# Token numbers of the expert slots from a DRAM table, tiles in pairs, an EPS column and moved work in a two-layer hybrid block

## The chip, the core and the metric

The kernel runs on one core of a Trainium2 chip. The metric is the device time of one execution in microseconds (us); less is better. Engines are named TensorE (PE in the rows; its weight loads are PEld), VectorE (DVE), ScalarE (ACT), GpSimd (POOL) and SyncE (SP). A "q" behind a name (ACTq) is the engine's own queue issuing something, such as a DMA.

## The reference

Input is a residual stream of 256 tokens of 1024 values, a conditioning vector, and the weights of two layers. All is float32. The layers have the same form, but the second one's channel part is a mixture of experts:

```python
def reference(x, c, ...):
    cond = silu(c)
    for l in range(2):
        sh_mix, sc_mix, gt_mix, sh_ffn, sc_ffn, gt_ffn = split(cond @ w_mod[l] + b_mod[l], 6)
        h = rms_norm(x, g_mix_pre[l]) * (1 + sc_mix) + sh_mix
        x = x + gt_mix * rms_norm(hybrid_mixer(h, ...), g_mix_post[l])   # two kinds of attention, 8 heads each
        h = rms_norm(x, g_ffn_pre[l]) * (1 + sc_ffn) + sh_ffn
        y = swiglu(h, w1, w3, w2) if l == 0 else moe_swiglu(h, w_router, w1, w3, w2)
        x = x + gt_ffn * rms_norm(y, g_ffn_post[l])

def moe_swiglu(h, w_router, w1, w3, w2):          # 8 experts, hidden width 3584
    top_v, top_i = top_k(h @ w_router, 2)
    combine = weights softmax(top_v) at top_i, else 0
    return sum(combine[:, e] * swiglu(h, w1[e], w3[e], w2[e]) for e in range(8))

def rms_norm(x, g):
    return x * rsqrt(mean(x * x) + EPS) * g
```

## The kernel before, in words

**Weights and products.** Weights come from DRAM in units of 1 MB into six `raw` buffers, issued by SyncE in a fixed order. Each unit is split into a high and a low part in float32r: ScalarE copies `raw` to `whi` (`split_hi`, L370), VectorE makes `wlo = raw - whi` (`split_lo`, L378), each in two halves of 128x1024. Three `whi`/`wlo` buffers turn round. TensorE forms every product from three (hi x hi, lo x hi, hi x lo: L1745, L1746, L1747 in `three`). Activations are split in the same way. SyncE may reload a `raw` buffer when VectorE has split what was in it.

**Order.** Each engine has its own program, written out by hand, and semaphores join them. An engine runs its program in order, so what stands behind a waiting instruction waits too. The stages are: first mixer, dense SwiGLU, second mixer, router, experts, final sum. Between stages, `transition` forms the RMS norms: ScalarE sums squares (`square_x`), GpSimd adds EPS (L1587) and raises to -1/2 (L1588, `rstd`), VectorE scales the rows (L935), TensorE transposes them (L1776).

**First stage.** For each of eight units, VectorE multiplies two halves of a modulation unit by the conditioning vector (`mod_columns`, L387), forms two coefficients (L952, L953), splits the unit's low part (L378 twice) and makes the low part of the hidden tile (`hlo`, L974) that TensorE's products with that unit need.

**Experts.** After the router, the work is cut into items: an item is one expert and up to 128 tokens. Eight items always run, and up to three more where an expert has over 128 tokens; in this run it is eight. Item 0 is written out, the others run in a loop whose count is read from memory. An item has seven blocks b of six units j: four for the two up products, two for the down product of the block before. In block b, ScalarE's `ffn_silu` (L777) and VectorE's `ffn_g` (L1260) make the hidden rows, TensorE transposes them (`hidden_T`, L2072) after unit 4.

**Tokens of an item.** `posI` holds, for each token and item, its slot. In block 2 of item n VectorE builds a 0/1 matrix of slots for item n+1 (`expert_slots`, L1377); in block 3 TensorE multiplies it with the token numbers (`slot_tokens`, L2252) and VectorE casts the result to `idx` (L1494). GpSimd then fetches the 128 rows of normed x from DRAM by `idx` (`fetch`, L1688). In blocks 4 and 5, TensorE transposes half of them each (`rows_T`, L2245), and ScalarE turns each half into four tiles of `h32e` (`tokens`, L854), between two unit splits.

**Sum.** An item's 128 output rows go to `y_rows` in DRAM (`store_rows`). In item 0 VectorE works out for each token the two rows of `y_rows` that are its own (`token_rows`, `ipair`, L1462); at the end GpSimd fetches them, and the last item is added from SBUF. Blocks of `y_rows` that no item may write are filled with zeros once, by a DMA that ScalarE issues (L868) after GpSimd has cleared its source (L1679).

## Time and profile before

| | |
|---|---|
| timed runs, median of 3 (lowest to highest) | 1620.96 us (1619.62 to 1623.14) |
| the profiled execution, its own time | 1618.41 us |
| its span, from first to last instruction | 1615.9 us |
| TensorE, VectorE, ScalarE, GpSimd busy | 1592.6, 1374.4, 1120.3, 142.8 us |
| expert items, 652 to 1560 us of the span | 908 us |

The profile is one execution of the program, so durations in it are compared with its own time, and only differences are carried over to the median. A busy share of TensorE says little by itself, since its products overlap; starts of instructions say more. "Idle before" names what ended the wait of an engine.

### The profile page before, as it was taken

Reading aid. Unit: us, or ns where it says so; the run is one execution under the profiler, and the core shown is the slowest. Engines: PE = TensorE matmul, PEld = TensorE weight load, DVE = VectorE, ACT = ScalarE, POOL = GpSimd, SP = SyncE. Lnnn points to the kernel's source line nnn. Section 1 sums busy time; section 2 is a strip of 40 time slices with the busy share of each in tenths; the row PEclk is TensorE's granted clock in tenths of the full one; section 3 lists DMA queues with packets and bytes.
Section 4 is the critical chain, followed back from the end, with each engine's and each line's share of the span. In section 5 each row is a group of like instructions: output and inputs, shape, how many; then the busy total and the mean of one; then the engine's idle time right before and its main releaser. Section 6 shows DMA issues by size and latency. Waiting matters only on the chain.

```text
span 1615.9 us, 23399 instructions
## 1 busy us (share of the span) xinstructions
PE 1592.6 (99%) x7726; PEld 1313.2 (81%) x7726; DVE 1374.4 (85%) x1661; ACT 1120.3 (69%) x1392; POOL 142.8 (9%) x214
## 2 busy tenths in 40 slices
PE   8999999999999999999999999999999999999997
PEld 7977878888789788788888888888888888888885
DVE  8888867787678767989988989989989989889898
ACT  5657544444456665778778778778878788788784
POOL 1030010000002100820000000000000000000071
PEclk9999999999999999999999999999999999999999
DMA  9966457777469453999999999999999999999993
GB/s 384 414 251 231 182 234 296 278 285 270 173 255 370 157 183 120 395 386 370 389 367 375 389 370 366 391 364 374 396 365 369 391 373 367 392 370 372 383 417 122
DMA packets 76409, 522.65 MB, mean 323 GB/s; under 512 B 9332, under 2 KB 10557, under 8 KB 14910
## 3 DMA queue, kind: packets, MB, share of 16 engines
q1 hardware_dynamic: 73522, 512.31, 81.7%
q0 software_dynamic: 1728, 6.29, 1.0%
q10 hardware_dynamic: 1100, 3.28, 0.5%
q8 instruction: 35, 0.57, 0.1%
q14 instruction: 24, 0.20, 0.0%
HBM read 513.97 MB, written 7.88 MB: 323 GB/s over the span
## 4 chain that ended last, share of the span: by engine, by line
PE 88%; DVE 4%; ACT 3%; issue 3%; POOL 0%; DMA 0%; DVEq 0%; ACTq 0%; POOLq 0%
PE ps L1745 27%; PE ps L1747 27%; PE ps L1746 27%; PE ps L2072 2%; DVE wlo L378 1%; ACT whi L370 1%; ACT vals L854 1%; DVE qk L1260 1%; PE ps L1800 1%; PE ps L1952 1%; PE ps L2245 0%; PE ps L1776 0%; PE ps L1931 0%; DVE raw L387 0%; DMA qk<-in_g_rows 0%
## 5 line engine op out<-in xcount | busy, mean ns | idle before, releaser
L378 DVE TENSOR_TENSOR wlo<-raw,whi 128x1024 fp32r<-128x1024 f32 x863 | 1014.5, 1227 | 141.5 <-ACT whi L370 141.0
L370 ACT ACTIVATE whi<-raw 128x1024 fp32r<-128x1024 f32 x863 | 862.8, 1053 | 202.3 <-PE ps L1747 178.8
L1745 PE MATMUL ps<-whi,hhi 128*128 128x512 f32 x1552 | 615.4, 397 | 2.3 <-DVE wlo L378 1.4
L1747 PE MATMUL ps<-wlo,hhi 128*128 128x512 f32 x1552 | 605.1, 390 | 0.0
L1746 PE MATMUL ps<-whi,hlo 128*128 128x512 f32 x1552 | 604.7, 390 | 0.0
L1745 PEld LDWEIGHTS ps<-whi,hhi 128*128 128x128 f32 x1552 | 291.4, 188 | 66.7 <-issue 4.4
L1747 PEld LDWEIGHTS ps<-wlo,hhi 128*128 128x128 f32 x1552 | 291.3, 188 | 62.2
L1746 PEld LDWEIGHTS ps<-whi,hlo 128*128 128x128 f32 x1552 | 291.7, 188 | 58.6 <-issue 1.0
L1745 PE MATMUL ps<-whi,ohi 128*128 128x512 f32 x432 | 173.2, 401 | 0.0
L1747 PE MATMUL ps<-wlo,ohi 128*128 128x512 f32 x432 | 168.9, 391 | 0.0
L1746 PE MATMUL ps<-whi,olo 128*128 128x512 f32 x432 | 168.4, 390 | 0.0
L387 DVE SCALAR_TENSOR_TENSOR raw<-raw,condb 128x1024 f32<-128x1024 f32 x94 | 111.5, 1223 | 0.0
L1747 PEld LDWEIGHTS ps<-wlo,ohi 128*128 128x128 f32 x432 | 81.1, 188 | 17.7
L1745 PEld LDWEIGHTS ps<-whi,ohi 128*128 128x128 f32 x432 | 81.2, 188 | 15.7 <-issue 0.3
L1746 PEld LDWEIGHTS ps<-whi,olo 128*128 128x128 f32 x432 | 81.3, 188 | 15.5
L777 ACT ACTIVATE qk<-ps 128x512 f32<-128x512 f32 x68 | 40.1, 598 | 61.5 <-PE ps L1747 61.5
L1745 PE MATMUL ps<-hhi,whi 128*128 128x256 f32 x256 | 73.8, 288 | 2.3 <-DVE hlo L974 2.3
L1687 POOL TENSOR_TENSOR spare<-tokid 128x1 f32<-128x1 f32 x8 | 2.0, 250 | 826.3 <-DVE idx L1494 826.3
L1746 PE MATMUL ps<-hhi,wlo 128*128 128x256 f32 x256 | 73.1, 285 | 0.0
L1747 PE MATMUL ps<-hlo,whi 128*128 128x256 f32 x256 | 73.0, 285 | 0.0
L782 ACT ACTIVATE ohi<-ps 128x512 fp32r<-128x512 f32 x46 | 27.5, 597 | 42.5 <-PE ps L2072 42.5
L1260 DVE TENSOR_TENSOR qk<-qk,ps 128x512 f32<-128x512 f32 x68 | 45.8, 681 | 10.8 <-PE ps L1747 10.8
(272 smaller groups left out, 1060.2 us busy)
## 6 DMA issues: line engine op xcount, KB each, us to landing
raw<-in_w_moe SPq DMA_DIRECT2D x336, 1024.0 KB, 7.1
raw<-in_w_pre_moe SPq DMA_DIRECT2D x97, 1024.0 KB, 5.0
raw<-in_w_mod_units SPq DMA_DIRECT2D x47, 1024.0 KB, 7.4
y_rows<-qk SPq DMA_DIRECT2D x7, 512.0 KB, 8.2
y_rows<-wide ACTq DMA_DIRECT2D x1, 2048.0 KB, 14.7
x<-in_x SPq DMA_DIRECT2D x2, 512.0 KB, 4.2
raw<-in_w_mod_units SPq DMA_DIRECT2D x2, 512.0 KB, 6.2
raw<-in_w_pre_moe SPq DMA_DIRECT2D x2, 512.0 KB, 7.7
```

The lines of the kernel that those rows point to most:

```text
L370: nc.scalar.activation(whi[:, home(s), part], raw[:, slot(s), part], ACT.Copy).then_inc(hi_done, 1)
L378: nc.vector.tensor_tensor(wlo[:, home(s), part], raw[:, slot(s), part], whi[:, home(s), part].bitcast(F32), ALU.subtract).then_inc(lo_done, 1)
L387: nc.vector.scalar_tensor_tensor(tile, tile, 1.0, condb[:], ALU.mult, ALU.mult, accum_out=modT[:, m:m + 1]).then_inc(mod_done, 1)
L777: nc.scalar.activation(silu[:, c, :], bank[c][:], ACT.Silu).then_inc(silu_done, 1)
L782: nc.scalar.activation(out, bank[6 + c][:].rearrange("p (k t) -> p k t", k=4), ACT.Copy).then_inc(gh_done, 1)
L854: nc.scalar.activation(h32e[:, k, :], src, ACT.Identity, scale=A[:, k:k + 1], bias=modT[:, SH[3] + k:SH[3] + k + 1]).then_inc(h32e_done, 1)
L1260: nc.vector.tensor_tensor(hid[:, c, :], silu[:, c, :], bank[(2 if n == 2 else 1) + c][:], ALU.mult)\
L1745: nc.tensor.matmul(out, a_hi, b_hi, start=first, stop=False, **kw)
L1746: nc.tensor.matmul(out, a_lo, b_hi, start=False, stop=False, **kw)
L1747: return nc.tensor.matmul(out, a_hi, b_lo, start=False, stop=last, **kw)
L1800: ins = nc.tensor.matmul(out, h32[:, k, c * P:(c + 1) * P], raw[:, slot(s0), k * NB:(k + 1) * NB], start=k == 0, stop=False)
L2072: ins = nc.tensor.transpose(bank[6 + c][:, k * P:(k + 1) * P], hid[:, c, k * P:(k + 1) * P], ident[:])
```

## The change

It has several parts, and what is computed stays the same.

1. **Slot numbers.** GpSimd scatters the token numbers 0 to 255 (`tokI`, four indirect DMAs of 128 words) to a DRAM table `tok_rows`, at the rows that `ipair` names, and reads it back as `idx_all`, one column for each item. ScalarE clears the table before by a DMA. In the looped items `idx` is a copy of a column; `expert_slots` and `slot_tokens` remain for item 0. So that a column is an item, `y_rows` and the table are laid out by slot and then item: a store's rows lie 12 rows apart. The zero fill covers five blocks of items, not four.
2. **Tiles in pairs.** ScalarE makes the four `h32e` tiles of a half in two pairs, one behind unit 2's split and one behind unit 3's.
3. **EPS column.** `x` gets a column 1025 that holds 32 times the root of EPS, so that the sum of squares holds EPS and GpSimd's add before `rstd` goes (not for the first norm, nor for the second half of the tokens before the router, nor for the last).
4. **Router.** The copies of `gate` from PSUM go from VectorE to ScalarE, behind the first item's splits; TensorE's gate transposes go behind the logits and filler takes their place. The logits product repeats the 8 columns 16 times.
5. **First stage.** `hlo` stands between the two low halves of a unit; unit 1's two modulation rows stand around unit 0's second low half; the copy of `distb` goes to ScalarE.

```diff
-        x = sb("x", [P, C, D])
+        x_eps = sb("x", [P, C, D + 1])
+        x = x_eps[:, :, 0:D]
...
+        tokI = sb("tokI", [P, C], mybir.dt.uint32)
+        idx_all = sb("idx_all", [P, ITEMS + 1], mybir.dt.uint32)
+        tok_table = tok_rows.rearrange("(p i) o -> p (i o)", p=P)
...
-                sp.dma_start(y_rows.rearrange("(i p) d -> i p d", p=P)[p], yrow).then_inc(yrow_free, 16)
+                sp.dma_start(y_rows.rearrange("(p i) d -> i p d", p=P)[p], yrow).then_inc(yrow_free, 16)
...
-                nc.scalar.activation(scr, x[:, c, :], ACT.Square, scale=1.0 / 32, accum_out=ss[:, 4 + c:5 + c])\
+                nc.scalar.activation(scr, x_eps[:, c, :], ACT.Square, scale=1.0 / 32, accum_out=ss[:, 4 + c:5 + c])\
...
-            def tokens(item, half):
+            def tokens(item, half, pair):
...
-                for k in range(4 * half, 4 * half + 4):
+                for k in range(4 * half + 2 * pair, 4 * half + 2 * pair + 2):
...
             split_hi(act, MOE0 + LEAD)
+            act.wait_ge(yg_done, 12)
+            for half in range(2):
+                act.wait_ge(gps_done, 2 * 3 + half + 1)
+                nc.scalar.activation(gate[:, half * NB:(half + 1) * NB], bank[GATE_BANK[3] + half], ACT.Copy).then_inc(gate_sb, 1)
             act.wait_ge(zero_set, 1)
-            act.dma_start(y_rows[(E - 1) * P:ITEMS * P, :].rearrange("(i p) d -> p i d", p=P),
-                          first_rows[:, 0:1, :].broadcast_to([P, EXTRA + 1, D])).then_inc(zero_out, 16)
+            act.dma_start(y_rows.rearrange("(p i) d -> p i d", p=P)[:, E - 1:ITEMS + 1, :],
+                          first_rows[:, 0:1, :].broadcast_to([P, EXTRA + 2, D])).then_inc(zero_out, 16)
+            act.wait_ge(tok_set, 2)
+            act.dma_start(tok_table, idx_all[:]).then_inc(table_zero, 16)
...
-                        if b in (4, 5) and j == 2:
+                        if b in (4, 5) and j in (2, 3):
                             act.wait_ge(elo_done, n * 2 + 2)
-                            tokens(n + 1, b - 4)
+                            tokens(n + 1, b - 4, j - 2)
...
                     if k:
-                        split_lo(dve, k)
+                        split_lo(dve, k, halves=(0,))
                         dve.wait_ge(eb_done, k)
...
                     if k == 0:
                         quarter(1, hi_done, lo_done)
+                        mod_columns(dve, 1, rows=(0,))
                         split_lo(dve, 0, halves=(1,))
-                        dve.wait_ge(dist_ps, 1)
-                        nc.vector.tensor_copy(distb[:, 0:DIST], bank[5][0:HEADS, 0:DIST]).then_inc(dist_sb, 1)
-                    if k + 1 < KC:
-                        mod_columns(dve, k + 1)
+                        mod_columns(dve, 1, rows=(1,))
+                    else:
+                        split_lo(dve, k, halves=(1,))
+                        if k + 1 < KC:
+                            mod_columns(dve, k + 1)
...
-                        if (b, j) == (2, 1):
-                            if p is None:
-                                dve.wait_ge(gath_done, 2)
-                            expert_slots(n + 1)
-                        if (b, j) == (3, 1):
-                            dve.wait_ge(idx_ps, n + 1)
-                            nc.vector.tensor_copy(idx[:], bank[7][:, S:S + 1]).then_inc(idx_sb, 1)
+                        if p is None and (b, j) == (2, 1):
+                            dve.wait_ge(gath_done, 2)
+                            expert_slots(1)
+                        if (b, j) == (3, 1):
+                            if p is None:
+                                dve.wait_ge(idx_ps, 1)
+                                nc.vector.tensor_copy(idx[:], bank[7][:, S:S + 1]).then_inc(idx_sb, 1)
+                            else:
+                                dve.wait_ge(table_in, 16)
+                                dve.wait_ge(gath_done, n * 2 + 2)
+                                nc.vector.tensor_copy(idx[:], idx_all[:, bass.ds(p + 2, 1)]).then_inc(idx_sb, 1)
...
             fetch(0)
+            pool.wait_ge(pair_done, 1)
+            pool.wait_ge(table_zero, 16)
+            pool.wait_ge(spare_set, 1)
+            nc.gpsimd.tensor_tensor(spare[:], tokid[:, 0:1], tokid[:, 1:2], ALU.add).then_inc(spare_set, 1)
+            for i in range(2):
+                for c in range(C):
+                    nc.gpsimd.indirect_dma_start(tok_rows, bass.IndirectOffsetOnAxis(ap=ipair[:, i * C + c:i * C + c + 1], axis=0),
+                                                 tokI[:, c:c + 1], None).then_inc(table_out, 16)
+            pool.wait_ge(table_out, 16 * 2 * C)
+            nc.gpsimd.dma_start(idx_all[:], tok_table).then_inc(table_in, 16)
...
                 if c:
-                    gate_rows(3)
+                    keep_busy(4)
                     transposes(3, c)
                 for k in range(KC):
                     pe.wait_ge(h32b if k >= 4 else h32a, KC * 2 + 4 * c + 4)
-                    ins = nc.tensor.matmul(bank[4][:, c * E:(c + 1) * E], h32[:, k, c * P:(c + 1) * P], wrA[:, k, :],
+                    ins = nc.tensor.matmul(bank[4][:, c * P:(c + 1) * P].rearrange("p (a e) -> p a e", e=E),
+                                           h32[:, k, c * P:(c + 1) * P],
+                                           wrA[:, k, :].rearrange("p (a e) -> p a e", a=1).broadcast_to([P, P // E, E]),
                                            start=k == 0, stop=k == KC - 1)
             ins.then_inc(lg_done, 1)
-            keep_busy(7)
+            gate_rows(3)
+            keep_busy(3)
...
-                        if (b, j) == (3, 0):
-                            slot_tokens(n)
+                        if p is None and (b, j) == (3, 0):
+                            slot_tokens()
```

The change moves line numbers; before and after are shown apart. ScalarE's program in a looped item, from block 4's `ffn_silu` on, where L370 (after: L379) is a split and L854 (after: L867) the tiles of `h32e`. Before:

```order
L777 ACTIVATE qk<-ps 128x512
L370 ACTIVATE whi<-raw 128x1024 x2
L905 ISA
L851 ISA
L854 ACTIVATE vals<-ps,modT,A 128x128 x4
L362 REGISTER_ALU
L370 ACTIVATE whi<-raw 128x1024 x2
```

After:

```order
L379 ACTIVATE whi<-raw 128x1024 x2
L924 ISA
L864 ISA
L867 ACTIVATE vals<-ps,modT,A 128x128 x2
L371 REGISTER_ALU
L379 ACTIVATE whi<-raw 128x1024 x2
L867 ACTIVATE vals<-ps,modT,A 128x128 x2
```

One unit split now stands between the two pairs of tiles. The second place is VectorE's program in the first stage, where L378 (after: L387) is a low half and L974 (after: L993) makes `hlo`. Before:

```order
L378 TENSOR_TENSOR wlo<-raw,whi 128x1024
L980 COPY qk<-ps 8x383
L387 SCALAR_TENSOR_TENSOR raw,modT<-raw,condb 128x1024 x2
L952 TENSOR_TENSOR modT<-modT,colsM 128x2
L953 SCALAR_TENSOR_TENSOR A<-modT,colsB 128x1
L378 TENSOR_TENSOR wlo<-raw,whi 128x1024 x2
L974 TENSOR_TENSOR hlo<-eb,hhi 128x256
```

After:

```order
L397 SCALAR_TENSOR_TENSOR raw,modT<-raw,condb 128x1024
L387 TENSOR_TENSOR wlo<-raw,whi 128x1024
L397 SCALAR_TENSOR_TENSOR raw,modT<-raw,condb 128x1024
L971 TENSOR_TENSOR modT<-modT,colsM 128x2
L972 SCALAR_TENSOR_TENSOR A<-modT,colsB 128x1
L387 TENSOR_TENSOR wlo<-raw,whi 128x1024
L993 TENSOR_TENSOR hlo<-eb,hhi 128x256
L387 TENSOR_TENSOR wlo<-raw,whi 128x1024
```

The copy has left, a modulation row stands ahead of the low half of unit 0, and `hlo` ahead of unit 1's second low half.

## Rows read from the trace of the kernel before

**Rows 1.** Page, part 1: busy us, share of the span, instructions.
```profile
PE 1592.6 (99%) x7726; PEld 1313.2 (81%) x7726; DVE 1374.4 (85%) x1661; ACT 1120.3 (69%) x1392; POOL 142.8 (9%) x214
```

**Rows 2.** Stretches: start:end, us, busy us of each engine, PEclk, DMA share, GB/s.
```profile
652.00:1560.00 908.00, 906.81 (x4130) 746.48 (x4129) 819.79 (x811) 733.46 (x841) 64.35 (x81) 1.00 0.98 380
```

**Rows 3.** ScalarE's waits, 652 to 1560 us: total, times, longest.
```profile
ACT whi L370 <- PE ps L1747: 68.6, 145, 0.7
```

**Rows 4.** DMA issues, 650 to 1590 us: count, KB each, median us to landing.
```profile
raw<-in_w_moe SPq DMA_DIRECT2D x327, 1024.0 KB, 7.1
y_rows<-qk SPq DMA_DIRECT2D x7, 512.0 KB, 8.2
```

**Rows 5.** Waits of TensorE's weight loads (PEld), 650 to 1590 us.
```profile
PEld ps L2072 <- DVE qk L1260: 8.9, 17, 1.0
```

**Rows 6.** Timeline, a token place: start us, us, instruction, idle before.
```profile
1312.82 1.50 ACT L854 ACTIVATE vals<-ps,modT,A 128x128 f32<-128x128 f32 x4 [0.67 <-PE ps L2245]
...
1315.31 2.36 DVE L378 TENSOR_TENSOR wlo<-raw,whi 128x1024 fp32r<-128x1024 f32 x2 [1.71 <-ACT whi L370]
...
1317.87 0.39 PE L1747 MATMUL ps<-wlo,ohi 128*128 128x512 f32 x1
...
1318.32 0.42 PEld L2072 LDWEIGHTS ps<-ident,qk 128*128 128x128 f32 x4 [0.48 <-DVE qk L1260]
...
1319.05 0.39 PE L1746 MATMUL ps<-whi,olo 128*128 128x512 f32 x1
```

**Rows 7.** Timeline, the same transposes where nothing is late.
```profile
1351.82 0.39 PE L1747 MATMUL ps<-wlo,ohi 128*128 128x512 f32 x1
...
1352.50 0.39 PE L1747 MATMUL ps<-wlo,ohi 128*128 128x512 f32 x1
...
1353.40 0.40 PE L1746 MATMUL ps<-whi,olo 128*128 128x512 f32 x1
```

**Rows 8.** Timeline, around the slot product L2252 (between the two).
```profile
810.65 0.39 PE L1747 MATMUL ps<-wlo,hhi 128*128 128x512 f32 x1
...
811.56 0.40 PE L1746 MATMUL ps<-whi,hlo 128*128 128x512 f32 x1
```

**Rows 9.** Tiles idx and ipair: ns min/median/max, first and last start us.
```profile
L1494 DVE CAST idx<-ps x8: 149/153/157, 696.7 to 1532.3; 128x1 uint32<-128x1 f32 x8
...
L1462 DVE CAST ipair<-rpair x1: 163/163/163, 747.6 to 747.6; 128x4 uint32<-128x4 f32 x1
```

**Rows 10.** Timeline, the zero fill's issue and what follows.
```profile
648.04 0.42 ACTq L868 DMA_DIRECT2D y_rows<-wide  x1
...
648.56 2.00 ACT L370 ACTIVATE whi<-raw 128x1024 fp32r<-128x1024 f32 x2 [3.27 <-POOL wide L1679]
...
651.00 0.50 PE L1745 MATMUL ps<-whi,hhi 128*128 128x512 f32 x1 [1.03 <-DVE wlo L378]
```

**Rows 11.** Timeline, weight loads of the logits and of the filler.
```profile
632.42 1.86 PEld L2214 LDWEIGHTS ps<-wrA,vals 128*128 128x128 f32 x16 [0.32 <-ACT vals L625]
...
634.20 1.64 PEld L2206 LDWEIGHTS ps<-nones,ones 128*128 128x128 f32 x14
```

**Rows 12.** Timeline, first stage, unit 1.
```profile
19.50 2.36 DVE L378 TENSOR_TENSOR wlo<-raw,whi 128x1024 fp32r<-128x1024 f32 x2
...
22.34 0.35 PE L1745 MATMUL ps<-hhi,whi 128*128 128x256 f32 x1 [0.90 <-DVE hlo L974]
```

**Rows 13.** Timeline, GpSimd's adds (L1587) and those who wait.
```profile
198.34 0.86 PEld L1776 LDWEIGHTS ps<-ident,wide 128*128 128x128 f32 x8 [0.38 <-DVE wide L935]
...
437.14 0.22 POOL L1587 TENSOR_SCALAR ss<-ss 128x1 f32<-128x1 f32 x1 [2.68 <-ACT at L586]
...
438.83 0.86 PEld L1776 LDWEIGHTS ps<-ident,wide 128*128 128x128 f32 x8 [0.74 <-DVE wide L935]
...
448.99 2.36 DVE L378 TENSOR_TENSOR wlo<-raw,whi 128x1024 fp32r<-128x1024 f32 x2
...
450.35 1.07 POOL L1587 TENSOR_SCALAR ss<-ss 128x1 f32<-128x1 f32 x1 [3.18 <-ACT at L586]
```

More of the change, by code:

```diff
@@ L1058, in router_transition @@
                                                accum_out=ss[:, 6:7]).then_inc(sqh_done, 1)
-                for half in range(2):
-                    gate_take(3, half)
             def last_add(i):
@@ L1441, in token_rows @@
                 if step == 2:
-                    link(nc.vector.tensor_tensor(row, place, jrow[:].rearrange("p (c i) -> p c i", c=1)
-                                                 .broadcast_to([P, C, ITEMS]), ALU.add))
+                    link(nc.vector.scalar_tensor_tensor(row, place, float(ITEMS + 1),
+                                                        jrow[:].rearrange("p (c i) -> p c i", c=1)
+                                                        .broadcast_to([P, C, ITEMS]), ALU.mult, ALU.add))
                 if step == 3:
@@ L1504, in _ @@
                 .then_inc(wcur_done, 1)
-            dve.wait_ge(cur_done, more + 3)
+            dve.wait_ge(cur_done, 3)
             slots_of(cur[:, 0, :])
@@ L1571, in _ @@
             links[0] += 1
+            nc.gpsimd.memset(x_eps[:, :, D:D + 1], 32 * EPS ** 0.5).then_inc(eps_set, 1)
             pool.wait_ge(pool_link, links[0])
@@ L1580, in _, with inv_rms @@
             select(lower, ALU.is_ge, -1, 1, 0, 0.0).then_inc(const, 1)
-            def inv_rms(done, src, at_col, *add):
+            def inv_rms(done, src, at_col, *add, with_eps=False):
                 if add:
                     link(nc.gpsimd.tensor_scalar(src, src, add[0], EPS, ALU.add, ALU.add))
-                else:
+                elif not with_eps:
                     link(nc.gpsimd.tensor_scalar(src, src, EPS, None, ALU.add))
```

43 lines of the change are left out of this document (27 added, 16 removed).

## The prediction, made before the run

> **What bounds the kernel now.** I read the page first: TensorE is busy for 99% of the span, VectorE for 85% [rows 1]. So what counts is TensorE's own work and the short gaps in it. The table of stretches puts 908 of the 1615.9 us into the expert items and shows TensorE full there, VectorE at 90%, ScalarE at 81%, and the DMA engines at 0.98 [rows 2]. The last figure asks whether the weight stream is the real bound. The list of waits answers no: ScalarE, which is the first to read each landed weight, waits in that stretch in six groups, all for TensorE, the largest being that for free whi buffers [rows 3]. No group names a DMA. A 1 MB load lands in 7.1 us [rows 4]; it is issued once unit s-6 has been split, about five unit periods of 2.8 us (1.05 MB at 380 GB/s [rows 2]) before ScalarE wants it. That leaves some 6 us.
>
> Then TensorE's gaps in the items: its weight loads wait for `ffn_g` (L1260) 17 times, 8.9 us in all, longest 1.0 [rows 5]. The timeline of one such place says why [rows 6]. ScalarE waits 0.67 us for the transposed rows, makes four h32e tiles in 1.50 us, and only then splits the next unit. VectorE's lo half of that unit starts after an idle of 1.71 us, `ffn_g` is queued behind it, and TensorE's hidden transposes load 0.48 us late.
>
> **The change part by part.** The sum is made against the profiled execution, 1618.41 us (span 1615.9), which lies 2.55 us under the median of the timed runs.
>
> *Token tiles in pairs.* What a gap costs is read from starts. From the last L1747 before the transposes to the L1746 behind them it is 1319.05-1317.87 = 1.18 us where `ffn_g` was late [rows 6], and 1353.40-1352.50 = 0.90 where it was not [rows 7]. So a listed idle of 0.48 costs 0.28; 0.20 of it is no loss. After the change two tiles stand ahead of the split, not four: half of 1.50, so the split, the lo half and `ffn_g` come 0.7 us earlier, 0.2 to 0.25 ahead of need. The other two tiles stand behind that split, so the split that follows them starts when it does now, and nothing is late next. Of the listed 8.9 us, 8.9-17x0.20 = 5.5 is real. One of the 17, in item 0, is at no token place and stays (0.3), and of the longest, 1.0, which the 0.7 doesn't cover, 0.1 stays: **-5.1 us**. Bounds: 0 (the lead is used up by something else) and 5.5.
>
> *Slot numbers from the table.* Item 0 keeps its product. In the seven looped items (y_rows is stored seven times [rows 4]) TensorE loses L2252. From L1747 to the L1746 behind it are 811.56-810.65 = 0.91 us [rows 8]; without it these are two steps of 0.227 us, a third of 1352.50-1351.82 [rows 7]. 7x(0.91-0.45) = **-3.2 us**; bounds 2.8 and 3.4. VectorE also loses a copy and two compares an item; it waits for ScalarE there, so I count nothing. What the table adds is on GpSimd's queue, behind the fetch for item 1: one small add, four scatters of 128 words, one read. GpSimd starts when `ipair` is ready, at 747.6; the first looped `idx` is wanted an item after the first, at 696.7+119.4 = 816 [rows 9]. No row shows a scatter of words. The 512 KB store lands in 8.2 us [rows 4]; four such in a row and a read are 41 us, which leaves 27. GpSimd's next fetch is queued behind them, and it too is wanted at 816 only. Cost 0, and to VectorE, which would wait, it costs only what goes beyond that.
>
> *A second DMA issue on ScalarE.* The zero fill of y_rows is issued at 648.04 in 0.42 us; before its next split ScalarE has been idle for 3.27 us, for GpSimd's memset, and TensorE then waits 1.03 us for the unit behind it [rows 10]. The table's clearing is issued in the same place: **+0.5 us** (0.42 and a gap). Bounds: 0, and 1.5 if five blocks take longer to issue than four. The two gate copies that move to ScalarE lie in the 3.27 us idle; without that cover they would cost their own length, which I put near the 1.50 us of the four tiles of [rows 6], the nearest row. Their reader on TensorE comes a block later.
>
> *Router.* The gate copies leave VectorE, but L1352, behind them, waits for the logits anyway. The logits product writes 128 columns for 8. The filler products of 128 columns took 1.64 us for 14 weight loads, the logits 1.86 for 16 [rows 11]: 0.117 each, so the loads pace both, and the width costs 0, at most 0.1. The gate transposes change places with filler: 0.
>
> *First stage.* TensorE waits 0.90 us for unit 1's `hlo`, which stands behind both lo halves, 2.36 together [rows 12]. Now it stands between them, 1.2 us earlier, so the gap goes. One mod row stands before unit 0's second lo half instead of behind it; that half is wanted only after two column blocks of products. The distb copy leaves VectorE. **-1.0 us**: the gap and a little fill. Bounds: 0 (that mod load lands late and holds VectorE, so that the unit after is late) and 1.1.
>
> *EPS column.* It removes one GpSimd add ahead of `rstd`. Where TensorE's loads wait 0.38 and 0.74 for the normed rows, less the 0.20 that is no loss, it gives 0.18 and, the add at 437.14 being 0.22 and its gap 0.08, 0.30 [rows 13]. The third add, at 450.35, took 1.07 us. But it ended just as VectorE's pair of L378 did, 448.99+2.36 = 451.35 [rows 13]: VectorE held it, and would hold the next GpSimd step in its place. So 0.2 there, not 1.1. **-0.7 us**, bounds 0 and 1.6.
> The Trainium skill says of this (page "SBUF — State Buffer", section "SBUF: two separate sides") that the two engines take a port pair as an exclusive lock for a whole instruction, and the loser blocks. By that rule the part is -0.7; by the add's length alone it would be -1.6.
>
> x[:, 1] now begins 4 bytes off. I count nothing for it; the last output transfer is the one place where it could show.
>
> Sum: -5.1-3.2+0.5-1.0-0.7 = -9.5 us. 1618.4-9.5 = 1608.9; against the timed median, 1620.96-9.5 = **1611.5 us**. Its own range goes from -11.6 (5.5, 3.4, 0, 1.1, 1.6) to -4.3 (half of the pairs, 2.8, 1.5 lost, half of the first stage): 1609.4 to 1616.7.
>
> **The rivals.**
> *The pairs don't free `ffn_g`.* The lead is 0.2 us, and the first pair still waits 0.67 us for the transposes. If VectorE has something else ahead of it, the waits stay: -9.5+5.1 = -4.4, 1616.6. For it: the small lead. Against: VectorE waited there for ScalarE, 1.71 us, and for nothing else.
> *The weight stream becomes the bound.* At 0.98 the DMA engines are nearly always busy [rows 2]. If they can't give more, an item stays as long as it is, and only the parts outside the items count: -1.0-0.7+0.5 = -1.2, 1619.8, no change. Against: no wait for a load in the stretch, 6 us in hand, and the demand rises by only 8.3/908 = 0.9%, from 380 to 384 GB/s.
> The Trainium skill's page "DMA: Bandwidth & Descriptors", section "Specifications", gives about 358 GB/s as one core's share of HBM. By that rule the stream would be over its limit already and this rival would hold, 1619.8; the trace disagrees, with 380 GB/s over 908 us.
> *Slower: the store with a stride.* y_rows is now slot-major, so a store writes rows of 4 KB that lie 48 KB apart. A store's share of the engines is 0.52 MB at 380 GB/s = 1.4 us. Free in an item are 2% of 119.4, 2.4 us, so it decides from 2.7 times the cost per row on. At four times it asks 4.2 more, 1.8 more than is free, in seven items: with the gain in the items gone too, 1620.96-1.2+12.6 = 1632. For it: the trace has no such store. Against: the packets stay 4 KB.
>
> **How the numbers follow.** Likeliest 0.68; pairs without effect 0.14; stream the bound 0.12; strided store 0.04; anything else 0.02. The predicted time is the first's, 1611.5. From 1607.5 (its low end and a run's spread, about 1.3 us under the median before) to 1617.5 (the first rival and the like) lie the first two cases, 0.82. A difference under 0.2% (3.2 us) can't be told from none: the first case and most of the second are faster, the third is the same. Faster 0.81, same 0.14, slower 0.05.
>
> **What would show each step.** Waits of TensorE's loads for `ffn_g` in the items: two or three for 17, under 2 us. No 128x1 product in looped items. An item of about 118.3 us for 119.4. TensorE starts unit 1 at about 21.3 us, not 22.34. The wait at 651 us is 1.5, not 1.03. At mixer 1's start `rstd` comes 0.2 to 0.3 earlier, its GpSimd row stretched by VectorE. I am wrong if ScalarE waits for raw in the items, if the waits for `ffn_g` stay, or if VectorE waits for the table.

## The result and the profile after

| | before | after |
|---|---|---|
| timed runs, median (lowest to highest) | 1620.3 us (1619.62 to 1623.14) | 1638.76 us (1638.3 to 1639.16) |
| span of the profiled execution | 1615.9 us | 1636.3 us |

The ratio is 1.0115, with a 95% interval from 1.0103 to 1.0127. The changed kernel is 18.5 us slower; the prediction was 1611.5 and faster, and the range ended at 1617.5.

First the page of the changed kernel, against [rows 1]: busy us, share of the span, instructions.

```profile
PE 1615.1 (99%) x7698; PEld 1310.0 (80%) x7698; DVE 1376.3 (84%) x1637; ACT 1121.6 (69%) x1395; POOL 152.0 (9%) x218
```

VectorE, ScalarE and the weight loads have the busy times of before to within 3.2 us. TensorE has 28 instructions fewer and 22.5 us more. The stretch of [rows 2] confirms it, now in the changed kernel:

```profile
652.00:1560.00 908.00, 906.57 (x4032) 732.78 (x4031) 808.71 (x782) 721.03 (x825) 65.40 (x91) 1.00 0.97 373
```

TensorE is as full as it was, at the same granted clock of 1.00, yet the stretch holds 4032 of its instructions where it held 4130. The DMA engines moved less, 373 GB/s for 380. So I looked for waits next. These are the ones of TensorE's weight loads in the changed kernel (the answer to [rows 5]; total, times, longest):

```profile
PEld ps L1781 <- DVE wlo L387: 1.9, 1, 1.9
PEld ps L2108 <- DVE qk L1279: 0.4, 1, 0.4
```

The 17 waits for `ffn_g` are one, where two or three were forecast. No wait has taken their place, and yet an item is longer: the tile `idx`, to be read beside [rows 9] (ns min/median/max, first and last start):

```profile
L1518 DVE COPY idx<-idx_all x7: 146/146/149, 823.6 to 1552.3; 128x1 uint32 x7
L1514 DVE CAST idx<-ps x1: 159/159/159, 703.3 to 703.3; 128x1 uint32<-128x1 f32 x1
```

(1552.3-823.6)/6 = 121.45 us an item for 119.4. What is left is the pace of the products themselves. The cleanest place is the dense SwiGLU, where the change moves nothing: 240 to 430 us, before,

```profile
240.00:430.00 190.00, 190.00 (x867) 157.23 (x866) 144.26 (x182) 77.99 (x89) 0.00 (x0) 1.00 0.74 279
```

and after:

```profile
240.00:430.00 190.00, 190.00 (x846) 153.63 (x845) 142.26 (x177) 77.77 (x89) 0.00 (x0) 1.00 0.73 276
```

TensorE never rests in either, and does 867 instructions in one and 846 in the other. The timeline of TensorE shows single products (start us, us; in `ps<-whi,hhi` the first name behind the arrow is the moving tile, the second the stationary one). Before:

```profile
901.67 0.39 PE L1745 MATMUL ps<-whi,hhi 128*128 128x512 f32 x1
...
903.48 0.39 PE L1747 MATMUL ps<-wlo,hhi 128*128 128x512 f32 x1
```

After:

```profile
901.67 0.39 PE L1782 MATMUL ps<-whi,hlo 128*128 128x512 f32 x1
...
903.53 0.40 PE L1781 MATMUL ps<-whi,hhi 128*128 128x512 f32 x1
```

Eight steps take 1.81 us before and 1.86 after. Over four windows of the trace (240 to 360, 700 to 760, 900 to 990, 1320 to 1410 us) I took the mean distance of the starts of consecutive 128x512 products, leaving out distances above 260 ns; this number is called **spacing** below. It is 227.3 to 227.7 ns before and 233.2 ns after, in every window. There are 3x1552 + 3x432 = 5952 such products, so 5.8 ns each are about 34.5 us, an estimate. The products with 256 columns did not slow down: behind the first 28 us of the trace they stand 119.9 ns apart before and 116.8 after, so a little closer. The weight loads take 188 ns both times.

The diff touches none of these products. What it does touch is where their operands lie in SBUF, the on-chip memory. `x` is allocated ahead of `hhi`, `hlo`, `ohi` and `olo`, and a row of it grew from 8192 to 8200 bytes, which the allocation rounds up to 8224. So all four stationary tiles (8192 bytes each) and all behind them lie 32 bytes further on, while `whi` and `wlo`, ahead of `x`, stay. Addresses in a partition, in bytes, as built:

| | whi | wlo | hhi | hlo |
|---|---|---|---|---|
| before | 65664 | 90240 | 127104 | 135296 |
| after | 65664 | 90240 | 127136 | 135328 |

### The profile page after: what moved, and what is told of

Its sections match the earlier page's. It is cut to its first block, busy times and chain, and to the rows that moved or that the text cites. A ratio compares the mean times of both kernels' runs of the same rounds, so it can differ in the third digit from the quotient of the medians.

```text
span 1636.3 us, 23335 instructions
## 1 busy us (share of the span) xinstructions
PE 1615.1 (99%) x7698; PEld 1310.0 (80%) x7698; DVE 1376.3 (84%) x1637; ACT 1121.6 (69%) x1395; POOL 152.0 (9%) x218
## 4 chain that ended last, share of the span: by engine, by line
PE 91%; DVE 3%; DMA 3%; ACT 1%; issue 1%; POOL 0%; ACTq 0%; DVEq 0%; POOLq 0%
PE ps L1781 29%; PE ps L1783 28%; PE ps L1782 28%; PE ps L2108 2%; DMA raw<-in_w_pre_moe 1%; DVE wlo L387 1%; DMA raw<-in_w_mod_units 1%; PE ps L1836 1%; ACT whi L379 1%; PE ps L1988 1%; DVE raw L397 0%; PE ps L2284 0%; PE ps L1812 0%; PE ps L1967 0%; DMA qk<-in_g_rows 0%
## 5 line engine op out<-in xcount | busy, mean ns | idle before, releaser
L387 DVE TENSOR_TENSOR wlo<-raw,whi 128x1024 fp32r<-128x1024 f32 x863 | 1020.2, 1229 | 150.3 <-ACT whi L379 149.3
L379 ACT ACTIVATE whi<-raw 128x1024 fp32r<-128x1024 f32 x863 | 864.4, 1052 | 219.5 <-PE ps L1783 194.0
L1781 PE MATMUL ps<-whi,hhi 128*128 128x512 f32 x1552 | 622.9, 401 | 2.3 <-DVE wlo L387 1.8
L1783 PE MATMUL ps<-wlo,hhi 128*128 128x512 f32 x1552 | 613.5, 395 | 0.0
L1782 PE MATMUL ps<-whi,hlo 128*128 128x512 f32 x1552 | 613.5, 395 | 0.0
```

The source lines that it names most:

```text
L379: nc.scalar.activation(whi[:, home(s), part], raw[:, slot(s), part], ACT.Copy).then_inc(hi_done, 1)
L387: nc.vector.tensor_tensor(wlo[:, home(s), part], raw[:, slot(s), part], whi[:, home(s), part].bitcast(F32), ALU.subtract).then_inc(lo_done, 1)
L1781: nc.tensor.matmul(out, a_hi, b_hi, start=first, stop=False, **kw)
L1782: nc.tensor.matmul(out, a_lo, b_hi, start=False, stop=False, **kw)
L1783: return nc.tensor.matmul(out, a_hi, b_lo, start=False, stop=last, **kw)
```

## The experiments

**Theory A**: the place of the stationary tiles against the moving ones sets the spacing; the parts of the change gave about what was forecast, and the 32 bytes took it and more. **Rival B**: the spacing follows from something that the change does (the second store layout, the table, x at odd places for its own readers), and the addresses are a coincidence. **Rival C**: the absolute alignment of a tile counts, not the distance between two.

### Where the tiles lie

The first four kernels share one edit, a tile `pad` that is never read, of 8 floats (32 bytes) unless said.

**e3_before_shift32** is the kernel before, with nothing else of the change:

```diff
+        pad = sb("pad", [P, 8])
         hhi = sb("hhi", [P, KC, S], F32R)
```

> The kernel before, with nothing but 32 unused bytes behind x. Theory A: 5952 x 5.4 ns = 32 us slower, about 1652 us, ratio 1.020, spacing 233 ns. Rivals B and C: no change, 1620.

Measured: 1645.33 us, ratio 1.0156 (1.0139 to 1.0173), spacing 233.2 ns. The same window as above, of this kernel:

```profile
240.00:430.00 190.00, 190.00 (x844) 153.56 (x843) 142.26 (x177) 78.18 (x89) 0.00 (x0) 1.00 0.73 277
```

32 unused bytes cost 24.6 us against the kernel before, and the window holds 844 instructions, 846 after the change. That ends rival B. The cost is under the estimate of 34.5 us. Set beside the trace of e6 below, which differs by the place of the pad alone, the distances between consecutive 128x512 products (5667 in e6, 5668 here) sum to 31.6 us more, the products with 256 columns give back 2.1, and the span is 25.8 longer. The rest, some 4 us, went into shorter waits and transposes. One such wait shows: the loads still wait for `ffn_g`, but 6.1 us in this kernel for the 8.9 of [rows 5]:

```profile
PEld ps L2073 <- DVE qk L1261: 6.1, 15, 0.5
```

**e4_before_shift32_behind** has the pad behind `olo`, so that only `wide`, `vals`, `qk` and the rest move.

```diff
+        pad = sb("pad", [P, 8])
         wide = sb("wide", [P, 2 * C * D])
```

> The kernel before, with the 32 unused bytes behind olo, so that hhi, hlo, ohi, olo (TensorE's stationary tiles) stay and wide, vals, qk and all later ones shift. If the stationary operand's address is the cause: no change, 1620. If it is traffic of the other engines on shifted tiles: about 1652.

Measured: 1619.94 us, ratio 0.9998 (0.9989 to 1.0008), spacing 227.3. So the move of `wide` and what follows costs nothing, and `hhi` to `olo` are left.

**e6_before_both32** has the pad ahead of `whi`: moving and stationary tiles shift together.

```diff
+        pad = sb("pad", [P, 8])
         whi = sb("whi", [P, SPLIT, UNIT], F32R)
```

> The kernel before with 32 unused bytes ahead of whi, so that moving and stationary tiles shift together by 32 bytes. If the distance between the two decides: no change, 1620, spacing 227.5. If the absolute address of the stationary tiles decides: 1645 as with the pad between them, spacing 233.

Measured: 1620.46 us, ratio 1.0 (0.999 to 1.0009), spacing 227.5. None of the six tiles lies where it did, and nothing is lost; `hhi` is at 127136, the very address that it has in e3. That ends rival C: the distance counts.

**e1_after_pad96** and **e2_after_pad32** ask the changed kernel how far is enough: pads of 96 and 32 bytes behind `x`, so that the tiles lie 128 and 64 bytes from their old place. e1 (e2 has 8 for 24):

```diff
+        pad = sb("pad", [P, 24])
         hhi = sb("hhi", [P, KC, S], F32R)
```

> The changed kernel with 96 unused bytes behind x, so that every tensor behind x starts again at a multiple of 128 bytes, as before the change. Theory A (the widened x moved all later tensors by 32 bytes, and TensorE's 128x512 products, whose stationary operand lies there, go from 227.5 to 233 ns apart): the spacing is 227.5 again, 5952 products give back 32 us, and the time is 1607 to 1610 us, ratio 0.992 to 0.994. Rival B (something the change computes or transfers slows TensorE): the time stays at 1638, spacing 233. Rival C (x[:, 1] off by 4 bytes slows its readers): stays at 1638 too.

> The changed kernel with 32 unused bytes behind x: later tensors start at odd multiples of 64 bytes. If theory A's grain is 64 bytes: 1607 to 1610 us like the 96-byte run. If it is 128 bytes: 1638, or between. Rivals B and C: 1638.

Measured: 1634.5 us (ratio 1.009, 1.0073 to 1.0106; spacing 232.4 to 232.8) with 128 bytes, and 1639.23 us (1.0119, 1.0102 to 1.0136; 233.3) with 64. My first idea, a line of 32, 64 or 128 bytes, was wrong.

**e13_before_shift256** is the kernel before with 256 bytes ahead of `hhi`.

```diff
+        pad = sb("pad", [P, 64])
         hhi = sb("hhi", [P, KC, S], F32R)
```

> The kernel before, with 256 bytes between x and hhi: all stationary tiles 256 bytes further from whi and wlo. Off by 32 and 64 bytes: 233.2 ns, by 128: 232.5 (in the changed kernel), by 512: 227.2. If the distance has to be a multiple of 256 bytes, 227.5 ns and 1620.4 us. If of 512 bytes: 232 ns and about 1640 us. If the effect fades with the distance: between, 229 to 231 ns, 1626 to 1635 us.

Measured: 1619.64 us, ratio 0.9999 (0.9989 to 1.0008), spacing 227.4. So the rule that fits all runs: a distance of a multiple of 256 bytes is good (256 more here, others in kernels below), and 32, 64 and 128 off are bad. Other remainders were not tried ahead of all four tiles. In the kernel before, whi to hhi is 61440 = 240x256.

### Which pair of tiles

**e14_shift_from_ohi** has the pad between `hlo` and `ohi`, **e11_shift_from_hlo** between `hhi` and `hlo`. **e15_only_hhi** puts `hhi` behind `olo`, with the pad ahead of it. **e16_only_wlo** puts the 32 bytes ahead of `wlo` and 224 behind it, so that `wlo` alone is off. The pads of e14, e11 and e16, and then the edit of e15:

```diff
+        pad = sb("pad", [P, 8])       # e14
         ohi = sb("ohi", [P, KC, S], F32R)
...
+        pad = sb("pad", [P, 8])       # e11
         hlo = sb("hlo", [P, KC, S], F32R)
...
+        pad = sb("pad", [P, 8])       # e16
         wlo = sb("wlo", [P, SPLIT, UNIT], F32R)
+        pad2 = sb("pad2", [P, 56])
         condb = sb("condb", [P, D])
```

```diff
-        hhi = sb("hhi", [P, KC, S], F32R)
         hlo = sb("hlo", [P, KC, S], F32R)
         ohi = sb("ohi", [P, KC, S], F32R)
         olo = sb("olo", [P, KC, S], F32R)
+        pad = sb("pad", [P, 8])
+        hhi = sb("hhi", [P, KC, S], F32R)
```

> The kernel before, with 32 bytes between hlo and ohi: only the stationary tiles of the down products, ohi and olo, are off (and wide and what follows, which e4_before_shift32_behind showed to be worth nothing). If a product is slow by the tiles that it and its neighbours use, the up products (hhi, hlo) stay at 227.5 ns and the down products (ohi, olo) go to 233: 1296 of 5952 products, 22% of the 24.5 us of e3_before_shift32, so 1620.4+5.3 = 1625.7 us (1624 to 1628). If any wrong tile slows all, 1645.

> The kernel before, with 32 bytes between hhi and hlo: hhi stays where it is, hlo, ohi, olo and what follows move by 32. If a product is slow when its own stationary tile lies wrong to its own moving tile, the products with hhi stay at 227.5 ns and those with hlo, ohi, olo have 233: the up products keep two thirds of their speed, the down products lose all, so two thirds of the 24.5 us of e3_before_shift32 or somewhat less: about 1633 us (1630 to 1637). If it is the load of the next stationary tile that collides with the stream that runs, the slow ones among the up products are those that precede a load from hlo, whatever their own tile. If only hhi's place matters, the time is that of the kernel before, 1620.5.

> The kernel before, with hhi moved behind olo and 32 bytes in front of it: hlo, ohi and olo lie at multiples of 4096 from whi, hhi does not; the mirror of e11_shift_from_hlo. If the load of a wrongly placed stationary tile disturbs the product that streams meanwhile, the intervals in which hhi is loaded (whi,hlo to wlo,hhi and wlo,hhi to whi,hhi) are slow and whi,hhi to whi,hlo stays fast, and the down products stay at 228 ns: spacing in the mean about 231 to 232, about 1636 us (1632 to 1642). If what counts is that the two stationary tiles in turn lie right to each other, the up products are slow by all three intervals, about 233 and 1640 us.

> The kernel before, with 32 bytes between whi and wlo and 224 bytes behind wlo: wlo is off by 32 to whi and by 224 to hhi, while whi to hhi is a multiple of 256. If 256 is a good distance (e13_before_shift256) and the stream of wlo is what a load then collides with, the products with wlo (a third) are slow and the others stay: about a third of 24.5 us, 1628 us (1626 to 1632). If only whi against the stationary tiles counts, 1620.4. If every wrong tile slows all, 1640 to 1645.

Measured: e14 1625.43 us (ratio 1.003, 1.0018 to 1.0041), e11 1647.45 (1.0163, 1.0147 to 1.0178), e15 1636.97 (1.0106, 1.0089 to 1.0122), e16 1638.09 (1.0112, 1.0095 to 1.0129). The timeline of the kernel before shows what goes on inside one interval, from one product's start to the next one's:

```profile
901.67 0.39 PE L1745 MATMUL ps<-whi,hhi 128*128 128x512 f32 x1
901.67 0.19 PEld L1746 LDWEIGHTS ps<-whi,hlo 128*128 128x128 f32 x1
901.90 0.39 PE L1746 MATMUL ps<-whi,hlo 128*128 128x512 f32 x1
```

The next product's stationary tile is loaded while the moving tile of the running one streams. The mean length of an interval by pair of products, over the whole trace, distances above 260 ns left out, in ns:

| interval | before | e3 | e11, hlo off | e15, hhi off | e16, wlo off | e14, ohi, olo off |
|---|---|---|---|---|---|---|
| whi streams, hlo loads | 227.6 | 233.3 | **238.3** | 230.6 | 229.6 | 227.4 |
| whi streams, hhi loads | 227.4 | 233.2 | 228.9 | **233.1** | 231.5 | 227.3 |
| wlo streams, hhi loads | 227.5 | 233.2 | 232.5 | **232.1** | **233.8** | 227.5 |
| whi streams, olo loads | 228.5 | 233.3 | **233.2** | 229.4 | 229.6 | **232.8** |

In bold stand the intervals in which the tile that streams and the tile that is loaded lie badly to each other (of e3 it is all four). Of the up products' three intervals, the one that rises most is a bold one in every kernel: by 10.7 in e11, 6.3 in e16, 5.7 in e15. A product's own stationary tile is not what counts, since in e11 the product with `hlo` has the fastest of the three (228.9). e14 is clean: up products keep their pace, down products lose 4.3 to 5.1 ns, and the time came within 0.3 us of what was expected. In the others the neighbours of a bad interval slow down too, by up to 5.0 ns in e11 (more than the 4.6 of a bad one in e15) and 4.1 in e16. So the mean rise over the three is 5.7 in e11, as in e3 where all lie badly, 4.4 in e15 and 4.1 in e16. The expectations for e11 (1633) and e16 (1628) counted bad pairs alone, and the times came out 14 and 10 us dearer. So the table points to TensorE's load of the next stationary tile meeting its own stream of the moving tile, and it doesn't show how a bad pair slows the interval behind it.

Do reads and writes of other engines take part? The traces at hand answer that. Take only the intervals in which ScalarE and VectorE are both idle throughout: 227.3 ns before (173 intervals), 233.1 after (183), and in e11 238.1, 228.6 and 232.5 in the order of the table's first three rows. That is the same as over all intervals. Nor is it the DMA engines. They stand still from 440 to 450 us, before and in e3:

```profile
440.00:450.00 10.00, 10.00 (x38) 6.77 (x36) 9.50 (x14) 7.36 (x13) 1.81 (x2) 1.00 0.00 0
440.00:450.00 10.00, 9.89 (x45) 7.37 (x44) 7.60 (x12) 7.49 (x13) 1.85 (x4) 1.00 0.00 0
```

and the consecutive 128x512 products there are 228.5 ns apart before (26 intervals) and 233.1 in e3 (30).

### The change with its tiles put right

**e5_x_behind** is the changed kernel with one allocation moved:

```diff
-        x_eps = sb("x", [P, C, D + 1])
-        x = x_eps[:, :, 0:D]
         hhi = sb("hhi", [P, KC, S], F32R)
...
         olo = sb("olo", [P, KC, S], F32R)
+        x_eps = sb("x", [P, C, D + 1])
+        x = x_eps[:, :, 0:D]
```

> The changed kernel with the wide x allocated behind olo. hhi, hlo, ohi, olo then lie 8192 bytes lower, so at the same place against whi and wlo modulo 8192 bytes, and only wide and all behind it stay shifted by 32. Theory A2 (what counts is where the stationary tiles lie against the moving whi and wlo, or against some large power of two, not their alignment to 32, 64 or 128 bytes; the 96-byte run left 232.4 ns): the spacing is 227.5 ns again and the time is what the prediction's sum gives, 1609 to 1612 us, ratio 0.993 to 0.995. Rival D (any move of the stationary tiles from where they were costs, by their absolute address): about 1635.

Measured: **1608.57 us**, ratio 0.9931 (0.9917 to 0.9944), spacing 227.2 to 227.5. The stretch of [rows 2] and the weight loads' waits:

```profile
652.00:1560.00 908.00, 908.00 (x4141) 751.59 (x4140) 826.49 (x796) 740.17 (x848) 83.34 (x86) 1.00 0.98 384
```

```profile
PEld ps L1781 <- DVE wlo L387: 3.9, 3, 2.1
PEld ps L2108 <- DVE qk L1279: 0.9, 1, 0.9
```

So the whole change is worth -11.8 us by the medians, and -9.7 by the two profiled executions (1618.41 and 1608.73). The kernel before scatters from 1618.3 to 1623.5 over all its timed runs, and its profiled execution lies at the low end; e12 below shows why.

**e9_condb_behind** also moves `condb` (4096 bytes) behind, which brings the tiles 4096 bytes nearer; **e10_ident_ahead** puts the 512 bytes of `ident` ahead of `hhi`. Both start from e5:

```diff
-        condb = sb("condb", [P, D])   # e9: from ahead of hhi to behind olo
         hhi = sb("hhi", [P, KC, S], F32R)
...
         olo = sb("olo", [P, KC, S], F32R)
+        condb = sb("condb", [P, D])
...
+        ident = sb("ident", [P, P])   # e10: from behind at2 to ahead of hhi
         hhi = sb("hhi", [P, KC, S], F32R)
```

> The kernel of e5_x_behind, but condb (4096 bytes, read only in the first stage and the modulation) is also taken out from between the weight tiles and the stationary tiles and stands behind olo: hhi to olo lie 4096 bytes nearer to whi and wlo, wide and what follows stay. If what counts is the distance modulo 4096 or less, the spacing of the 128x512 products stays 227.5 ns and the time is that of e5_x_behind, about 1608.6 us (1607.5 to 1610). If it counts modulo 8192, the spacing is 233 ns and the time about 1638. If a whole multiple of 8192 is better still than an odd multiple of 4096, the spacing falls under 227 ns, and each ns less is worth up to 6 us.

> The kernel of e5_x_behind, but the 512-byte tile ident stands ahead of hhi: hhi to olo and all up to ident's old place lie 512 bytes further from whi and wlo. Distances of 32 and 64 bytes off gave 233.2 ns, 128 off gave 232.5, both beside 227.5 for a multiple of 4096. If only the low bits up to 256 bytes count, this one is as fast as e5_x_behind, 1608.6 us (1607 to 1610.5). If the distance must be a multiple of 4096, it is slow: 232 to 233 ns, about 1634 to 1638 us. A value between, 229 to 231 ns and 1615 to 1628 us, would say that the effect fades with the distance.

Measured: 1608.6 us (ratio 0.9928, 0.9912 to 0.9943) and **1608.03 us** (0.9923, 0.9908 to 0.9938), spacing 227.3 and 227.2. Both are good distances; e10 is the fastest kernel of the study, by no more than can be told from e5.

### What each part is worth

Three kernels take one part out of e5. **e7_no_pairs** puts the four `h32e` tiles of a half back behind one split:

```diff
-                for k in range(4 * half + 2 * pair, 4 * half + 2 * pair + 2):
+                for k in range(4 * half, 4 * half + 4):
...
-                        if b in (4, 5) and j in (2, 3):
+                        if b in (4, 5) and j == 2:
```

> The x-behind kernel with all four h32e tiles ahead of the split again (part 2 of the change undone). By the prediction it is 5.1 us slower than the x-behind kernel and TensorE's loads wait some 15 times for ffn_g, 0.5 us each. If the pairs do nothing: the same as x-behind.

Measured: 1613.75 us, e5 plus 5.2 (ratio to before 0.9961, 0.9948 to 0.9974). The waits are back, as the wait row of this kernel shows:

```profile
PEld ps L2108 <- DVE qk L1279: 8.9, 16, 1.3
```

**e8_products_back** makes `idx` in every item by `expert_slots` and `slot_tokens` again; the table is still written and waited for.

```diff
-                        if p is None and (b, j) == (2, 1):
-                            dve.wait_ge(gath_done, 2)
-                            expert_slots(1)
+                        if (b, j) == (2, 1):
+                            if p is None:
+                                dve.wait_ge(gath_done, 2)
+                            expert_slots(n + 1)
...
-                                nc.vector.tensor_copy(idx[:], idx_all[:, bass.ds(p + 2, 1)]).then_inc(idx_sb, 1)
+                            nc.vector.tensor_copy(idx[:], bank[7][:, S:S + 1]).then_inc(idx_sb, 1)
...
-                        if p is None and (b, j) == (3, 0):
-                            slot_tokens()
+                        if (b, j) == (3, 0):
+                            slot_tokens(n)
```

> The x-behind kernel with the slot matrix and the product with the token numbers made in every item again and idx taken from them; the table is still written and waited for, but not read. By the prediction it is 3.2 us slower than the x-behind kernel (0.46 us in each of seven items). If the product was hidden: the same.

Measured: 1612.77 us, e5 plus 4.2 (ratio 0.9957, 0.9942 to 0.9973); by spans, 1609.9 and 1606.7, plus 3.2.

**e12_first_stage_back** undoes part 5 (ScalarE's copy of `distb` goes too):

```diff
-                        split_lo(dve, k, halves=(0,))
+                        split_lo(dve, k)
...
-                        mod_columns(dve, 1, rows=(0,))
                         split_lo(dve, 0, halves=(1,))
-                        mod_columns(dve, 1, rows=(1,))
-                    else:
-                        split_lo(dve, k, halves=(1,))
-                        if k + 1 < KC:
-                            mod_columns(dve, k + 1)
+                        dve.wait_ge(dist_ps, 1)
+                        nc.vector.tensor_copy(distb[:, 0:DIST], bank[5][0:HEADS, 0:DIST]).then_inc(dist_sb, 1)
+                    if k + 1 < KC:
+                        mod_columns(dve, k + 1)
```

> The kernel of e5_x_behind with part 5 of the change (first stage: hlo between the halves, modulation rows around, copy of distb on ScalarE) undone. The prediction's term for this part was -1.0 us. Then this kernel has 1609.6 us. If the part is what carried the 2.4 us that the other terms leave of the 11.8, it has 1610.5 to 1611. If the part is worth nothing, 1608.6.

Measured: 1610.94 us, e5 plus 2.4 (ratio 0.9937, 0.9924 to 0.9951). In the timelines of TensorE, unit 1 of the first stage starts in e12 at

```profile
22.59 0.55 PE L1777 MATMUL ps<-hhi,whi 128*128 128x256 f32 x1 [2.39 <-DVE hlo L991]
```

and in e5 at

```profile
21.18 0.36 PE L1781 MATMUL ps<-hhi,whi 128*128 128x256 f32 x1 [0.64 <-DVE hlo L993]
```

The stretch from 22.5 to 25.5 us, e12,

```profile
22.50:25.50 3.00, 2.91 (x14) 2.94 (x14) 2.90 (x7) 1.64 (x3) 0.00 (x0) 0.50 1.02 423
```

and e5:

```profile
22.50:25.50 3.00, 3.00 (x21) 2.77 (x21) 2.90 (x7) 2.62 (x4) 0.00 (x0) 1.00 1.04 429
```

After 2.39 us of idling TensorE had a granted clock of 0.50, which is 1.2 GHz, where e5 after 0.64 us had 1.00. The kernel before idled 0.90 us there in its profile [rows 12], and one could think that the undo costs more than the part gave. But the old first stage goes in two ways. e6 is the kernel before with a pad that costs nothing, and its profiled execution idles 2.39 us as e12 does. Its first products of unit 0, and where unit 1 starts:

```profile
14.35 0.28 PE L1747 MATMUL ps<-hhi,wlo 128*128 128x256 f32 x1
14.46 0.28 PE L1748 MATMUL ps<-hlo,whi 128*128 128x256 f32 x1
...
22.47 0.36 PE L1746 MATMUL ps<-hhi,whi 128*128 128x256 f32 x1 [2.39 <-DVE hlo L975]
```

The same products of unit 0 in the profile of the kernel before:

```profile
14.39 0.41 PE L1746 MATMUL ps<-hhi,wlo 128*128 128x256 f32 x1
14.61 0.41 PE L1747 MATMUL ps<-hlo,whi 128*128 128x256 f32 x1
```

There they stand 0.21 us apart up to 17.4 us, for 0.12 in e6. Unit 1 waits for `hlo` and starts at nearly the same time in both (22.34 and 22.47), so the slow pace only fills the wait. What follows differs. The stretch from 22.5 to 25.5 us, before and in e6:

```profile
22.50:25.50 3.00, 3.00 (x25) 2.98 (x26) 2.90 (x7) 1.74 (x4) 0.00 (x0) 1.00 1.00 418
22.50:25.50 3.00, 3.00 (x16) 3.00 (x17) 2.90 (x7) 1.70 (x3) 0.00 (x0) 0.58 1.02 426
```

The span of e6 is 1617.9 us for 1615.9. Of the ten profiled executions with the old first stage, three idle 0.89 to 0.91 us (before, e4, e13) and seven 2.39 to 2.41 (e3, e6, e11, e12, e14, e15, e16). The timed runs of the kernel before that were taken beside the experiments fall into two groups too, 17 from 1618.29 to 1619.58 and 37 from 1620.04 up. The profiled executions of before, e4 and e13 have times like the first (1617.98 to 1618.43), that of e6 like the second (1620.38). Two of e12's five runs, 1609.47 and 1609.63, are 0.9 to 1.1 above e5, the other three 2.4 to 2.7. So part 5 is worth some 1.1 us against an execution like the profiled one (unit 1 starts at 21.18 for 22.34 us, 1.16 earlier) and 1.5 to 2 us more against the commoner kind, whose clock falls. That the groups of times are these two ways fits, but only the profiled executions show it.

## Why the prediction was wrong

**The step that failed** is the one that began "x[:, 1] now begins 4 bytes off. I count nothing for it". It asked what a wider `x` does to those who read `x`, and looked no further than the last output transfer. It did not ask what lies behind `x` in SBUF. The 5952 products whose own code did not change were taken at their old 0.227 us, the very step length from [rows 7] that the sum used; they had 0.233. No rival named it either: the slower one was the strided store at 1632, and its signs are absent. A store lands in 7.9 us in the changed kernel, for the 8.2 of [rows 4]:

```profile
y_rows<-qk SPq DMA_DIRECT2D x7, 512.0 KB, 7.9
```

e3 gives the price of the missed step in the kernel before, +24.6 us. In the changed kernel it is 1638.76-1608.57 = +30.2. More of it shows there: of 32.5 us that the distances between consecutive 128x512 products grow by from e5 to the changed kernel, 29.6 appear in the span; of 31.6 from e6 to e3, 25.8. The changed kernel has fewer waits that slower products could shorten.

**With the tiles put right, the sum holds.** It said -9.5 us against the profiled execution; e5 has -9.7 there. Its time, 1608.57, lies in the predicted range, 2.9 under 1611.5. The sum was carried over to the median of before as if nothing but noise lay between it and the profile; most executions of the old first stage also pay for a fall of the clock (e12), which the change takes away. By its terms:

- *Pairs*, -5.1: right. 5.2 us by e7 (4.9 by spans), and one wait for `ffn_g` instead of the "two or three". The first rival is refuted: a lead of 0.2 us was enough.
- *Slot table*, -3.2: right by spans (3.2), 4.2 by medians; the runs don't tell these apart. What GpSimd does for the table costs nothing: VectorE's list of waits has none for the table, and e5 has both the table and the gain.
- *Second issue on ScalarE*, +0.5: right. In e5 TensorE waits 1.65 us for the unit behind it, for the 1.03 of [rows 10], with two issues ahead of the split. Timeline, ScalarE's queue and TensorE:

```profile
646.57 0.43 ACTq L885 DMA_DIRECT2D y_rows<-wide  x1
...
647.04 0.55 ACTq L888 DMA_DIRECT2D tok_rows<-idx_all  x1
647.69 2.00 ACT L379 ACTIVATE whi<-raw 128x1024 fp32r<-128x1024 f32 x2 [2.91 <-issue]
...
650.14 0.50 PE L1781 MATMUL ps<-whi,hhi 128*128 128x512 f32 x1 [1.65 <-DVE wlo L387]
```

- *First stage*, -1.0: right as against the profiled execution of before (1.16 us, start forecast at "about 21.3", found at 21.18). By medians it is 2.4 (e12). The gap of 0.90 us, from which the term was read, was the smaller of the two kinds; the longer gap with the fall of the clock behind it is in no row of before.
- *EPS column*, -0.7: no run takes this part alone, but the rows bear it out. In e5 TensorE's loads no longer wait at the first place (0.38 before) and wait 0.42 at the second, at 437.61 us, for the 0.74 of before. The sign that was named is there. In e5 the third place reads, against [rows 13]:

```profile
449.14 1.41 POOL L1615 TENSOR_TENSOR rstd<-ss,nhalf 128x1 f32<-128x1 f32 x1 [3.20 <-ACT at L599]
450.58 0.75 DVE L954 TENSOR_SCALAR wide<-x,rstd 128x1024 f32<-128x1024 f32 x1 [0.44 <-POOL rstd L1615]
...
451.48 1.06 PE L1812 MATMUL ps<-ident,wide 128*128 128x128 f32 x8 [0.76 <-DVE wide L954]
```

GpSimd's add is gone, and the power step in its place took 1.41 us; the same step took 0.55 at 436.22, with no pair of low halves beside it. Here VectorE's pair ran from 447.78 to 450.14, and GpSimd ended 0.41 us behind it. TensorE waits 0.76 us there, and before it waited 1.06:

```profile
452.99 0.74 PE L1776 MATMUL ps<-ident,wide 128*128 128x128 f32 x5 [1.06 <-DVE wide L935]
```

That is 0.3 of the 1.07 of the add, near what the sum took (0.2), not the whole. The exclusive port pair of the Trainium skill's page "SBUF — State Buffer", section "SBUF: two separate sides", describes this row too.
- *Weight stream as the bound*: refuted. e5 moves 384 GB/s over the same 908 us at a share of 0.98, exactly the demand that was worked out.
- *Router*: no run isolates it.

## What to carry to other kernels

A change to the size of one tile moves every tile allocated behind it, so list the addresses of TensorE's operands before and after, keep the distances from moving to stationary tiles, and put tiles whose size may change behind them. When a result doesn't fit, compare first the count of instructions in a stretch that the change doesn't touch and in which TensorE never waits: 867 against 846 shows that the pace of TensorE's own products changed, which no list of waits does. And look at more than one execution of the kernel before: a gap read from its single profile was the rarer of two kinds.

## What the runs showed of the hardware

- The pace of products of 128x512 in float32r, each with a weight load of its own, depends on the distance in bytes between the moving and the stationary tile: 227.1 to 227.7 ns in every window for multiples of 256 (240x256 before and in e6; that plus 256, minus 8192, minus 7680 and minus 12288 in e13, e5, e10 and e9), 232.4 to 232.8 at 128 off, 233.2 to 233.3 at 32 and 64 off. It is the same with ScalarE and VectorE idle (227.3 and 233.1). The Trainium skill's page "SBUF — State Buffer", section "SBUF: two separate sides", says that TensorE's ports never wait on anyone. Whether a port waits here the runs don't show, but at equal busy share and clock the pace differs by 2.5%. Its page "TensorE: Matmul & The Clock Gate", section "Wait — 56ns, not 53.3ns?", has 215.7 ns from start to start at 512 columns; these kernels, with other data and a load for each product, don't come below 227 in any window.
- For products with 256 columns (there `hhi` and `hlo` stream, `whi` and `wlo` are loaded) it is the other way round, and small: 119.9 ns apart before, 116.8 in e3 and the changed kernel, 118.9 in e1. There are 768 of them, so some 2 us, an estimate.
- Slower products shorten waits: of the 31.6 us by which the distances between consecutive 128x512 products grow from e6 to e3, 25.8 appear in the span; from e5 to the changed kernel it is 29.6 of 32.5.
- In the first stage, an idle time of 2.39 to 2.41 us was followed by a mean granted clock of 0.50 to 0.74 from 22.5 to 25.5 us (e3, e6, e11, e12, e14, e15, e16), and one of 0.89 to 0.91 by 1.00 (before, e4, e13). In those three, products ahead of it had stood 0.21 us apart for some 3 us, for 0.12 in the others. e4 and e13 show 0.53 granted from 15 to 18 us; the profile of before shows 1.00 at that very pace, so its clock row can't be relied on there. Why they were slow is open.
